# The last seam of a fused two-block kernel: the operand of up3 made from the output and a premultiplied residual, its pieces four tiles wide, up3 over six PSUM banks

## The chip, the cores and the metric

The kernel runs on one core of a Trainium2 chip. The metric is the device time of one launch in microseconds (us), lower is better. The engines are called by their short names: PE is TensorE, DVE is VectorE, ACT is ScalarE, POOL is GpSimd, SP is the engine that issues most transfers.

## What is computed

Two transformer-like blocks, one after the other, on 256 tokens of width 1024, all in float32. The change touches the place between the token mixer of the second block and its last feed-forward half:

```python
xs = xs + mod_x[5] * rmsnorm_2(y, g[3])          # y is the product with w_o ("o2")
xs = ffn_half(xs, mod_x[6], mod_x[7], mod_x[8], g[4], g[5], w_ff_in[l, 1], w_ff_out[l, 1])

def ffn_half(s, shift, scale, gate, g_pre, g_post, w_in, w_out):
    h = swiglu(modulate(rmsnorm_2(s, g_pre), shift, scale), w_in, w_out)
    return s + 0.5 * gate * rmsnorm_2(h, g_post)
```

So the output y of o2 is normalised and scaled by a gain row (g0 below), the residual is added, and the new residual is normalised, scaled by a second gain row (g1), turned to channels-major and multiplied with `w_ff_in` ("up3", 44 slabs of 128 columns: gate and up alternate) and then with `w_ff_out` ("down3").

## The kernel before

Every weight matrix comes as slabs of 128x1024 float32. For slab s, ACT rounds the raw slab into `hi` (the helper `split` on ACT) and DVE writes the remainder into `lo` (the helper `split` on DVE). Activations are held as `nh` and `nl` in the same way, and PE makes each product from three matmuls: nh*hi, nh*lo, nl*hi. There are HL = 3 slots of hi and lo, so slab s+3 can be split once slab s is used, and five slots of raw slabs, which SP fills in ring order. Nothing is scheduled automatically: each engine runs its instructions in the order in which the code issues them, and semaphores hold it where it has to wait. PE waits for `lo_done` before each slab (`begin`).

In the stage o2, the output has tokens on the partitions: PSUM banks 0 and 1 hold the two halves of token tile 0, banks 2 and 3 those of tile 1. The last two slabs of o2 are run bank by bank (`row_tail`), so that bank 0 is done first. For each bank, ACT squares it (`output_square`, a sum over the row comes with it); for each token tile ACT takes a root and DVE the inverse.

Before the change, DVE then multiplies each bank with g0 (`gained`), adds it with the inverse to the residual `xr` (`added_row`), and the new residual is multiplied with g1 into `xgr`: tile 0 by POOL, tile 1 by DVE (`next_gain`). PE transposes `xgr` in six pieces (`turned_rows`), ACT rounds each piece into `nh` (`pieces_rounded`) and DVE takes the remainder into `nl` (`piece_remainders`). The inverse norm of the new residual is not in that operand. It is applied to up3's results: ACT squares the new residual (`residual_square`), DVE makes a diagonal matrix of the inverse (`diagonal`), and PE multiplies it with ones (`inverse_rows`), which leaves the inverse in PSUM, along the columns (semaphore `stat`). DVE copies that to `rinv` and can only then take up3's first results. That is in `up` on DVE, and `up` on ACT holds the matching steps. Which slab these issue a split for, and where, matters here. In both kernels the split of slab 4 of up3 is issued in `up` of slab 1: on DVE behind all that takes in slabs 0 and 1, on ACT behind Silu of slab 0; and that Silu waits until DVE has multiplied slab 0 with `rinv`.

A second place is named below. Towards the end of the woven stage (positions p = 34 to 39 of its slabs), DVE scales the attention output `otok` (its line 2076, 128x2048), PE transposes pieces of it (`turn_out`, line 2789), and DVE takes the remainders of these pieces (line 2040, semaphore `o_lo`, on which the turns from the fourth on wait). POOL starts the transfer that broadcasts the gain rows g0, g1, g2 into `gain_rows` (line 686), which waits for the attention's last product.

Of the kernel before, what the change touches and what calls it, by code (L numbers as in the profile page):

```python
# [13 lines left out]
P = 128  # L14
D = 1024
# [6 lines left out]
BANKS = 4  # L22
# [31 lines left out]
def constants():  # L54
# [69 lines left out]
    "xg": dict(ffn1=2, pre2c=8, pre2x=6, mod2x=8, mod2c=8, rows2=2),  # L124
    "nh": dict(mix1=8, ffn1=6, pre2c=8, pre2x=8, mod2x=4, mod2c=4, pre3=7),
    "nl": dict(mix1=8, ffn1=6, pre2c=8, pre2x=8, mod2x=4, mod2c=4, pre3=7),
    "piece_made": dict(ffn1=6, pre2x=4, mod2x=4, mod2c=4, pre3=6),
# [30 lines left out]
PIECES_OF_PAIR = (2, 3, 5, 6)  # L158
# [58 lines left out]
def plan():  # L217
# [21 lines left out]
    st["up3"] = stage_slabs("up3", 2 * KH, cols=T + 2)  # L239
# [19 lines left out]
    for s, x in enumerate(work):  # L259
# [5 lines left out]
        if x.name == "v2" or x.name in ROWS:  # L265
            x.uses = list(uses)
            if x.j % 4 == 3 if x.name == "v2" else x.last:
                uses = [n + 1 for n in uses]
        else:
            x.use = uses[x.bank]  # L270
            uses[x.bank] += x.last and x.name != "in1"
# [7 lines left out]
def build(nc, d, out):  # L279
    st, work, ring = plan()  # L280
    with ExitStack() as ctx:
# [131 lines left out]
        squares = place(100 * KB, "squares", [P, 2, 512])  # L413
        diag = place(105 * KB, "diag", [P, 2, P])
# [41 lines left out]
        bank_free = [sem(f"bank_free{b}") for b in range(BANKS)]  # L456
# [54 lines left out]
        def _(pool):  # L511
# [178 lines left out]
            for b in range(2):  # L690
                w = slice(b * 512, b * 512 + 512)
                pool.wait_ge(sem("x"), since("x", "rows2") + b + 1)
                pool.tensor_tensor(xgr[:, 0, w], xr[:, 0, w], gain_rows[:, 1, w], ALU.mult)\
                    .then_inc(sem("xg_pool"), 1)


        @block.scalar
        def _(act):
# [14 lines left out]
            def prime(n, func):  # L713
                act.activation(idle[:, n:n + 1], cc("one"), func).then_inc(sem("primed"), 1)
# [62 lines left out]
            def pieces_rounded(m, between):  # L777


                if m == "pre3":  # L780

                    act.wait_ge(slab_used, st["o2"][-1].s + 1)
                    act.activation(nh[:, :, T:T + 2], mod[:, 6 * KD:7 * KD, 0:1].broadcast_to([P, KD, 2]), ACT.Copy)\
                       .then_inc(sem("nh"), 1)
                for n, (bank, k0, kn, tt) in enumerate(PIECES):
                    act.wait_ge(sem("piece_made"), since("piece_made", m) + n + 1)
# [3 lines left out]
                    if between and n == 1:  # L790
                        between()
# [18 lines left out]
            act.activation(idle[:, 6:7], small[:, 0:1], ACT.Copy).then_inc(sem("primed"), 1)  # L810
# [44 lines left out]
            for x in st["in1"]:  # L855
# [38 lines left out]
                if p == 10:  # L894
                    act.wait_ge(sem("c_landed"), 16)
                    act.activation(cvec[:, :, :], cvec[:, :, :], ACT.Silu).then_inc(sem("c_ready"), 1)
                    act.wait_ge(sem("u1_done"), Z1 + 3)
                    act.activation(u1[:, Z1:Z1 + 3, :], u1[:, Z1:Z1 + 3, :], ACT.Silu)\
                       .then_inc(sem("z_ready"), 1)
# [22 lines left out]
                if p == 17:  # L922
                    act.wait_ge(sem("ystat_ready"), 1)
                    act.activation(yroot[:, :, :], streams(ps[:, 5, :]), ACT.Sqrt, scale=1.0 / 192,
                                   bias=cc("eps")).then_inc(sem("yroot_ready"), 1)
# [41 lines left out]
            pieces_rounded("ffn1", None)  # L967
# [247 lines left out]
            for name in WOVEN:  # L1215
                for x in st[name]:
# [36 lines left out]
                    if p == 34:  # L1253
                        act.wait_ge(sem("oss_ready"), 2 * HEADS2)
                        act.activation(small[:, 208:224], small[:, 192:208], ACT.Sqrt, scale=1.0 / P,
                                       bias=cc("eps")).then_inc(sem("oroot_ready"), 1)
# [23 lines left out]
            for tt in range(2):  # L1280
                output_square(tt, 0)
                output_square(tt, 1)
                row_root("rows2", tt, tt + 1, 2 * tt + 2, SUM + 2 * tt + 1, PART + tt, ROOT + tt)
            residual_square(0, 0)
            split(st["o2"][-2].s + HL)
            pieces_rounded("pre3", None)
            split(st["o2"][-1].s + HL)
            residual_square(0, 1)
            row_root("rows2", 2, 3, 6, SUM + 5, PART + 2, ROOT + 2)
            residual_square(1, 0)  # L1290
# [18 lines left out]
        def _(dve):  # L1309
# [138 lines left out]
            def piece_remainders(m):  # L1448
# [1480 lines left out]
```

## Time and profile before

| | |
|---|---|
| median of 3 runs | 1268.71 us (1268.59 to 1270.02) |
| span of the profiled execution, from the first to the last instruction | 1265.3 us |
| median less that span | 3.4 us |
| PE busy, share of the span | 98% |
| DVE, ACT, POOL busy | 70%, 46%, 8% |
| mean granted clock of PE, share of full speed | 0.997 |

The profiled execution has no time of its own beside its span; the 3.4 us between the span and the median are what lies around the instructions. An engine's line in a timeline gives start, duration, engine, source line and operation, the tile written and those read, and in brackets how long the engine was idle before it and which instruction ended that. Durations of neighbouring instructions overlap a little, since each engine is pipelined.

### The profile page before, as it was taken

To read this page: it belongs to the slowest core of one execution; us is meant where nothing else is said; L and a number is where in the kernel's file an instruction comes from. 1 tells how busy PE (TensorE), PEld (TensorE's weight loads), DVE (VectorE), ACT (ScalarE), POOL (GpSimd) and SP (SyncE) were. 2 spreads that over 40 slices of the span, in tenths; PEclk is the share of its full clock that TensorE was granted. 3 is DMA by queue.
4 is the path that set the end of the run, shared out by engine and by line. 5 is a ranking of instruction groups with operands and counts; after the bars stand their busy time and mean duration, and the time that the engine had idled before them with its cause. 6 is when DMAs were issued, how large, how long until landed. Compare 5 with 4: busy or idle time off the path is not lost.

```text
span 1265.3 us, 19254 instructions
## 1 busy us (share of the span) xinstructions
PE 1235.7 (98%) x7645; PEld 1089.6 (86%) x7645; DVE 882.9 (70%) x1439; ACT 585.8 (46%) x927; POOL 100.6 (8%) x103
## 2 busy tenths in 40 slices
PE   6999999999999999999999999999999998999997
PEld 6987999978888888887787998888789997999986
DVE  5986889797787777753425776367886676777744
ACT  7656545545622222322325752246355645544533
POOL 2130001000000000001100022011420000000000
PEclk9999999999999999999999999999999999999999
DMA  7644777777366678853332543333233554655562
GB/s 288 209 139 150 233 235 242 234 242 238 112 217 200 199 251 282 293 189 107 110 133 75 167 150 100 100 117 116 86 101 100 200 167 139 193 180 181 179 195 84
DMA packets 59753, 219.28 MB, mean 173 GB/s; under 512 B 6844, under 2 KB 7136, under 8 KB 58896
## 3 DMA queue, kind: packets, MB, share of 16 engines
q1 hardware_dynamic: 56736, 205.42, 50.0%
q0 software_dynamic: 2352, 11.76, 2.7%
q8 instruction: 61, 1.00, 0.3%
q10 hardware_dynamic: 576, 0.88, 0.2%
q14 instruction: 28, 0.23, 0.1%
HBM read 216.95 MB, written 1.07 MB: 172 GB/s over the span
## 4 chain that ended last, share of the span: by engine, by line
PE 85%; DVE 6%; ACT 5%; issue 2%; DMA 1%; POOL 0%; DVEq 0%; ACTq 0%
PE ps L2182 19%; PE ps L2184 18%; PE ps L2183 18%; PE ps L2230 4%; PE ps L2232 4%; PE ps L2231 4%; PE ps L2241 3%; PE ps L2243 3%; PE ps L2242 3%; ACT hi L711 2%; PE ps L2220 1%; PE ps L2218 1%; PE ps L2219 1%; PE ps L2766 1%; DVE lo L1347 1%
## 5 line engine op out<-in xcount | busy, mean ns | idle before, releaser
L1347 DVE TENSOR_TENSOR lo<-raw,hi 128x1024 fp32r<-128x1024 f32 x315 | 388.5, 1234 | 247.5 <-ACT hi L711 244.4
L2182 PE MATMUL ps<-nh,hi 128*128 128x256 f32 (+2 forms) x1776 | 552.0, 311 | 4.5 <-DMA con<-in_consts 1.7
L711 ACT ACTIVATE hi<-raw 128x1024 fp32r<-128x1024 f32 x315 | 333.1, 1058 | 474.0 <-PE ps L2184 277.0
L2183 PE MATMUL ps<-nh,lo 128*128 128x256 f32 (+2 forms) x1776 | 544.2, 306 | 0.0
L2184 PE MATMUL ps<-nl,hi 128*128 128x256 f32 (+2 forms) x1776 | 544.1, 306 | 0.0
L2182 PEld LDWEIGHTS ps<-nh,hi 128*128 128x128 f32 x1776 | 338.4, 191 | 35.2 <-issue 15.7
L2183 PEld LDWEIGHTS ps<-nh,lo 128*128 128x128 f32 x1776 | 338.5, 191 | 16.5 <-issue 1.2
L2184 PEld LDWEIGHTS ps<-nl,hi 128*128 128x128 f32 x1776 | 338.3, 190 | 15.1
L1334 DVE SCALAR_TENSOR_TENSOR raw<-raw,cvec 128x1024 f32<-128x1024 f32 x72 | 86.8, 1222 | 1.4
L2230 PE MATMUL ps<-hi,H 128*128 128x512 f32 x176 | 69.1, 392 | 1.1 <-DVE lo L1347 1.1
L2241 PE MATMUL ps<-hi,H 128*128 128x512 f32 x176 | 69.4, 394 | 0.2 <-DVE ygx L1826 0.2
L2243 PE MATMUL ps<-hi,H 128*128 128x512 f32 x176 | 68.6, 390 | 0.0
L2231 PE MATMUL ps<-lo,H 128*128 128x512 f32 x176 | 68.5, 389 | 0.0
L2232 PE MATMUL ps<-hi,H 128*128 128x512 f32 x176 | 68.5, 389 | 0.0
L2242 PE MATMUL ps<-lo,H 128*128 128x512 f32 x176 | 68.5, 389 | 0.0
L1383 DVE TENSOR_TENSOR sg<-sg,ps 128x256 f32<-128x256 f32 (+1 forms) x44 | 24.3, 553 | 50.8 <-PE ps L2184 50.3
L1329 DVE SCALAR_TENSOR_TENSOR ps<-raw,cvec 128x1024 f32<-128x1024 f32 x40 | 49.0, 1226 | 0.0
L733 ACT ACTIVATE sg<-ps 128x512 f32<-128x512 f32 x22 | 13.1, 597 | 72.3 <-PE ps L2184 72.3
L2241 PEld LDWEIGHTS ps<-hi,H 128*128 128x128 f32 x176 | 33.0, 188 | 9.7 <-issue 2.9
L2230 PEld LDWEIGHTS ps<-hi,H 128*128 128x128 f32 x176 | 33.0, 188 | 9.5 <-DVE lo L1347 1.9
L1194 ACT ACTIVATE p<-ps,small 128x512 f32<-128x512 f32 x32 | 21.7, 684 | 41.3 <-DVE small L1994 41.3
L2243 PEld LDWEIGHTS ps<-hi,H 128*128 128x128 f32 x176 | 33.0, 188 | 7.0
(384 smaller groups left out, 1381.8 us busy)
## 6 DMA issues: line engine op xcount, KB each, us to landing
raw<-in_up SPq DMA_DIRECT2D x132, 512.0 KB, 3.7
raw<-in_in SPq DMA_DIRECT2D x86, 512.0 KB, 3.6
raw<-in_w_ada SPq DMA_DIRECT2D x72, 512.0 KB, 4.5
raw<-in_down SPq DMA_DIRECT2D x66, 512.0 KB, 3.7
raw<-in_out SPq DMA_DIRECT2D x8, 512.0 KB, 3.6
raw<-in_hy_out SPq DMA_DIRECT2D x8, 512.0 KB, 3.6
raw<-in_da_out SPq DMA_DIRECT2D x8, 512.0 KB, 4.0
raw<-in_o SPq DMA_DIRECT2D x8, 512.0 KB, 3.5
```

What stands on the lines that cost most here:

```text
L711: act.activation(hi[:, h, 0:n], raw[:, r, 0:n], ACT.Copy).then_inc(hi_done, 1)
L1334: dve.scalar_tensor_tensor(w, w, 1.0, cx, ALU.mult, ALU.mult, accum_out=mod[:, m:m + 1, s])\
L1347: dve.tensor_tensor(lo[:, h, 0:w], raw[:, r, 0:w], hi[:, h, 0:w].bitcast(F32), ALU.subtract).then_inc(lo_done, 1)
L2182: mm(o, hi[:, h, wk], x_hi, start=first, stop=False)
L2183: mm(o, lo[:, h, wk], x_hi, start=False, stop=False)
L2184: return mm(o, hi[:, h, wk], x_lo, start=False, stop=last)
L2230: mm(ps[:, b, :], x_hi, hi[:, h, w], start=x.first, stop=False)
L2231: mm(ps[:, b, :], x_hi, lo[:, h, w], start=False, stop=False)
L2232: return mm(ps[:, b, :], x_lo, hi[:, h, w], start=False, stop=x.last)
L2241: mm(ps[:, tt, :], x_hi, hi[:, h, w], start=x.first and j == 0, stop=False)
L2242: mm(ps[:, tt, :], x_hi, lo[:, h, w], start=False, stop=False)
L2243: o = mm(ps[:, tt, :], x_lo, hi[:, h, w], start=False, stop=x.last and j == 1)
```

## The change

1. POOL, once the gain rows have landed, multiplies g0 by g1 (`both_rows`, 128x1024) and the old residual by g1 into `xgr` (two instructions of 128x1024).
2. At the end of o2 DVE multiplies each bank with g0*g1 (`both_gained`, into `ygg`) and makes up3's operand as ygg * inverse + xgr (`next_operand`). The residual itself (`gained`, `added_row`) is made later, between the splits of up3's slabs. One of the four g0 products is done otherwise: ACT copies bank 1 to `yg` and POOL multiplies it.
3. PE transposes four pieces of four tiles each, in banks 4 to 7 (`turned_tiles`); ACT rounds them (`tile_rounded`), DVE takes the remainders in the order 0, 2, 1, 3 (`tile_remainders`).
4. up3 uses six banks (0, 1, 2, 3, 5, 6) and PE makes the inverse rows after four slabs of up3 (`x.j == 3`), not after two (`x.j == 1`).
5. The split of slab 3 of up3 is issued before `up`, in the seam; the split of slab 4 stays where it was, in `up` of slab 1.
6. Some semaphores are merged or dropped (`silu_done`, `root_ready`, `primed`).

```diff
-BANKS = 4
+BANKS = (0, 1, 2, 3, 5, 6)
...
+PIECES3 = ((4, 0, 0), (5, 4, 0), (6, 0, 1), (7, 4, 1))
+LOWS3 = (0, 2, 1, 3)
...
             pool.wait_ge(sem("gain_rows_landed"), 112)
-            for b in range(2):
-                w = slice(b * 512, b * 512 + 512)
-                pool.wait_ge(sem("x"), since("x", "rows2") + b + 1)
-                pool.tensor_tensor(xgr[:, 0, w], xr[:, 0, w], gain_rows[:, 1, w], ALU.mult)\
+            pool.tensor_tensor(both_rows[:, :], gain_rows[:, 0, :], gain_rows[:, 1, :], ALU.mult)\
+                .then_inc(sem("xg_pool"), 1)
+            pool.wait_ge(sem("yhy_ready"), KD)
+            for tt in range(2):
+                pool.tensor_tensor(xgr[:, tt, :], xr[:, tt, :], gain_rows[:, 1, :], ALU.mult)\
                     .then_inc(sem("xg_pool"), 1)
+            pool.wait_ge(bank_free[1], st["o2"][-1].uses[1] + 1)
+            pool.wait_ge(sem("xg"), since("xg", "rows2") + 4)
+            pool.tensor_tensor(yg[:, 0, 512:D], yg[:, 0, 512:D], gain_rows[:, 0, 512:D], ALU.mult)\
+                .then_inc(sem("xg_pool"), 1)
...
@@ ACT, up
-                    split(x.s + HL)
+                    if x.name == "up1" or x.j:
+                        split(x.s + HL)
...
@@ ACT, the seam
+            output_square(0, 0)
+            output_square(0, 1)
+            output_root(0)
+            output_square(1, 0)
+            act.wait_ge(sem("both_gained"), 2)
+            act.activation(yg[:, 0, 512:D], ps[:, 1, :], ACT.Copy).then_inc(bank_free[1], 1)
+            output_square(1, 1)
+            output_root(1)
+            shift_rounded()
+            tile_rounded(0)
+            split(st["o2"][-2].s + HL)
+            tile_rounded(1)
+            split(st["o2"][-1].s + HL)
             residual_square(0, 0)
...
+            split(st["up3"][0].s + HL)
+            residual_square(1, 0)
...
@@ DVE, up
-                    split(x.s + HL)
+                    if x.name == "up1":
+                        split(x.s + HL)
...
+            def both_gained(b):
+
+
+                dve.wait_ge(sem("sq"), since("sq", "rows2") + b + 1)
+                dve.tensor_tensor(piece(ygg, b), ps[:, b, :], both_rows[:, b % 2 * 512:b % 2 * 512 + 512],
+                                  ALU.mult).then_inc(sem("both_gained"), 1)
...
@@ PE
             for x in fed(st["up3"], "pre3"):
-                if x.j == 1:
+                if x.j == 3:
                     inverse_rows(2)
```

The change moves instructions on DVE, ACT, PE and POOL. First POOL, at the end of its program: the rows of the kernel before (names as in the code; `waits` lists the semaphores).

```order
L683 TENSOR_TENSOR proj<-proj 128x2x256 [waits folded]
L681 TENSOR_TENSOR ut<-spec_im 128x512
L683 TENSOR_TENSOR spec_im<-spec_im 128x2x256 [waits folded]
L686 DMA gain_rows<-gain_mem 128x3072 [waits o2_ready]
L693 TENSOR_TENSOR xgr<-xr,gain_rows 128x512 [waits x,gain_rows_landed]
L693 TENSOR_TENSOR xgr<-xr,gain_rows 128x512 [waits x]
L281 UNCONDITIONAL_BRANCH
```

And of the changed kernel, from the same transfer on:

```order
L691 DMA gain_rows<-gain_mem 128x3072 [waits o2_ready]
L695 TENSOR_TENSOR both_rows<-gain_rows 128x1024 [waits gain_rows_landed]
L699 TENSOR_TENSOR xgr<-xr,gain_rows 128x1024 [waits yhy_ready]
L699 TENSOR_TENSOR xgr<-xr,gain_rows 128x1024
L703 TENSOR_TENSOR yg<-yg,gain_rows 128x512 [waits xg,bank_free1]
L284 UNCONDITIONAL_BRANCH
```

Three instructions of 128x1024 now run as soon as the gain rows land, where before POOL was idle until the residual of the seam was there.

Next DVE in the seam, from the last split of o2 to the transposed pieces, in the kernel before:

```order
L1347 TENSOR_TENSOR lo<-raw,hi 128x1024 [waits hi_done] x5
L1405 TENSOR_SCALAR small<-small 128x1 [waits sq]
L2107 TENSOR_TENSOR yg<-ps,gain_rows 128x512 [waits sq] x2
L1410 RECIPROCAL small<-small 128x1 [waits root]
L2115 SCALAR_TENSOR_TENSOR xr<-yg,small,xr 128x512 [waits bank_free0,rinv]
L2115 SCALAR_TENSOR_TENSOR xr<-yg,small,xr 128x512 [waits bank_free1,rinv]
...
L2120 TENSOR_TENSOR xgr<-xr,gain_rows 128x512 [waits x] x2
L1453 TENSOR_TENSOR nl<-mod,nh 128x8x2 [waits nh]
L1458 TENSOR_TENSOR nl<-ps,nh 128x4x128 [waits nh]
```

In the changed kernel:

```order
L1378 TENSOR_TENSOR lo<-raw,hi 128x1024 [waits hi_done] x5
L1437 TENSOR_SCALAR small<-small 128x1 [waits sq,xg_pool]
L2164 TENSOR_TENSOR ygg<-ps,both_rows 128x512 [waits sq]
L2149 TENSOR_TENSOR yg<-ps,gain_rows 128x512 [waits sq]
L2164 TENSOR_TENSOR ygg<-ps,both_rows 128x512 [waits sq]
L1442 RECIPROCAL small<-small 128x1 [waits root]
L2172 SCALAR_TENSOR_TENSOR xgr<-ygg,small,xgr 128x512 [waits both_gained,rinv] x2
...
L2164 TENSOR_TENSOR ygg<-ps,both_rows 128x512 [waits sq] x2
L1442 RECIPROCAL small<-small 128x1 [waits root]
L2172 SCALAR_TENSOR_TENSOR xgr<-ygg,small,xgr 128x512 [waits both_gained,rinv] x2
L1491 TENSOR_TENSOR nl<-mod,nh 128x8x2 [waits nh]
L1501 TENSOR_TENSOR nl<-ps,nh 128x4x128 [waits nh] x4
```

The row L2120 between the new residual and the transposes is gone, and so is POOL's work there.

Last DVE between the second diagonal and the first splits of up3. Before (`diag` is the diagonal, `sg` the gate, COPY rinv is the first to wait for `stat`):

```order
L1445 TENSOR_SCALAR diag<-con,small 128x128 [waits rinv]
L1347 TENSOR_TENSOR lo<-raw,hi 128x1024 [waits hi_done]
L1358 COPY rinv<-ps 128x256 [waits stat]
L1363 COPY small<-ps 128x1 [waits slab_used,dve_step]
L1364 TENSOR_TENSOR sg<-ps,rinv 128x256
L1370 COPY small<-ps 128x1 [waits slab_used]
L1371 TENSOR_TENSOR sg<-ps,rinv 128x256
L1374 SCALAR_TENSOR_TENSOR sg<-sg,small 128x256 [waits gate_open,dve_step]
L1347 TENSOR_TENSOR lo<-raw,hi 128x1024 [waits hi_done]
```

In the changed kernel:

```order
L1477 TENSOR_SCALAR diag<-con,small 128x128 [waits rinv]
L1390 COPY rinv<-ps 128x256 [waits stat]
L1395 COPY small<-ps 128x1 [waits slab_used,dve_step]
L1396 TENSOR_TENSOR sg<-ps,rinv 128x256
L1402 COPY small<-ps 128x1 [waits slab_used]
L1403 TENSOR_TENSOR sg<-ps,rinv 128x256
L1406 SCALAR_TENSOR_TENSOR sg<-sg,small 128x256 [waits gate_open,dve_step]
L1378 TENSOR_TENSOR lo<-raw,hi 128x1024 [waits hi_done]
```

The first `lo` of the rows before is the split of slab 3 of up3 and has moved up into the seam; the second is that of slab 4, and it still stands behind the row that waits for `stat`.

## Rows read from the trace of the kernel before

**Rows 1.** The page: busy us, share of the span, instructions.

```profile
PE 1235.7 (98%) x7645; PEld 1089.6 (86%) x7645; DVE 882.9 (70%) x1439; ACT 585.8 (46%) x927; POOL 100.6 (8%) x103
```

**Rows 2.** Timeline of PE in the seam, from the last matmul of o2.

```profile
1061.86 0.39 PE L2232 MATMUL ps<-hi,nl 128*128 128x512 f32 x1
1063.77 0.63 PE L2307 MATMUL ps<-con,xgr 128*128 128x128 f32 x4 [1.52 <-POOL xgr L693]
1066.73 2.82 PE L2307 MATMUL ps<-con,xgr 128*128 128x128 f32 x12 [2.33 <-DVE xgr L2120]
1069.20 0.56 PE L2182 MATMUL ps<-nh,hi 128*128 128x258 f32 x1
...
1069.99 0.32 PE L2182 MATMUL ps<-nh,hi 128*128 128x258 f32 x1
```

**Rows 3.** Timeline of ACT in the seam.

```profile
1060.92 0.60 ACT L758 ACTIVATE squares<-ps 128x512 f32<-128x512 f32 x1 [0.28 <-PE ps L2232]
...
1063.06 0.29 ACT L766 ACTIVATE small<-small 128x1 f32<-128x1 f32 x1
...
1064.93 0.57 ACT L787 ACTIVATE nh<-ps 128x512 fp32r<-128x512 f32 x1
```

**Rows 4.** Timeline of DVE in the seam.

```profile
1059.14 0.15 DVE L1405 TENSOR_SCALAR small<-small 128x1 f32<-128x1 f32 x1
...
1061.08 1.41 DVE L2115 SCALAR_TENSOR_TENSOR xr<-yg,small,xr 128x512 f32<-128x512 f32 x2
...
1062.48 1.28 DVE L2107 TENSOR_TENSOR yg<-ps,gain_rows 128x512 f32<-128x512 f32 x2
```

**Rows 5.** Stretches of time: busy us by engine, then granted clock, DMA.

```profile
1062.30:1069.20 6.90, 3.10 (x16) 2.90 (x17) 6.39 (x13) 4.35 (x11) 2.56 (x2) 0.81 0.00 0
1066.60:1070.00 3.40, 3.27 (x16) 3.27 (x17) 2.76 (x8) 2.04 (x6) 0.00 (x0) 0.50 0.02 5
123.00:127.00 4.00, 2.88 (x21) 2.13 (x20) 3.97 (x8) 3.87 (x10) 0.57 (x1) 1.00 0.08 31
1261.00:1263.00 2.00, 0.00 (x0) 0.00 (x0) 1.24 (x3) 0.00 (x0) 0.00 (x0) 0.55 0.35 129
```

**Rows 6.** Timeline of PE around the inverse rows (L2315).

```profile
1075.42 0.61 PE L2315 MATMUL ps<-diag,con 128*128 128x128 f32 x4
1075.79 0.36 PE L2182 MATMUL ps<-nh,hi 128*128 128x258 f32 x1
```

**Rows 7.** Timeline of DVE and ACT, from the copy of rinv on.

```profile
1077.47 0.42 DVE L1358 COPY rinv<-ps 128x256 f32<-128x256 f32 x1
...
1078.87 1.04 ACT L711 ACTIVATE hi<-raw 128x1024 fp32r<-128x1024 f32 x1
1079.94 1.23 DVE L1347 TENSOR_TENSOR lo<-raw,hi 128x1024 fp32r<-128x1024 f32 x1 [0.39 <-ACT hi L711]
```

**Rows 8.** The gain rows' transfer (KB, us to landing), and who then works.

```profile
994.53 0.58 POOL L686 DMA_DIRECT2D gain_rows<-gain_mem  x1 [63.50 <-PE ps L2745]
gain_rows<-gain_mem POOLq DMA_DIRECT2D x1, 1536.0 KB, 8.6
1003.60 2.29 DVE L2076 TENSOR_TENSOR otok<-otok,small 128x2048 f32<-128x2048 f32 x1
1005.95 0.66 PE L2789 MATMUL ps<-con,otok 128*128 128x128 f32 x4 [0.21 <-DVE otok L2076]
...
1012.62 0.60 PE L2789 MATMUL ps<-con,otok 128*128 128x128 f32 x4
```

**Rows 9.** Timeline of POOL and DVE where both run at once.

```profile
757.62 1.29 POOL L658 TENSOR_TENSOR kre<-kre 128x512 f32<-128x512 f32 x1
758.30 1.68 DVE L1347 TENSOR_TENSOR lo<-raw,hi 128x1024 fp32r<-128x1024 f32 x1 [1.92 <-ACT hi L711]
...
900.95 2.22 POOL L681 TENSOR_TENSOR ut<-proj 128x512 f32<-128x512 f32 x1
901.94 1.39 DVE L1986 CUSTOM_DVE_ANT_0 rtmp<-otok 128x128 f32<-128x128 f32 x1
```

More of the change, by code:

```diff
@@ L238, in plan @@
     st["o2"] = row_slabs_of("o2", KD)
-    st["up3"] = stage_slabs("up3", 2 * KH, cols=T + 2)
+    st["up3"] = stage_slabs("up3", 2 * KH, cols=T + 2, banks=BANKS)
     st["down3"] = row_slabs_of("down3", KH)
@@ L413, in build @@
         squares = place(100 * KB, "squares", [P, 2, 512])
+        both_rows = place(82 * KB, "both_rows", [P, D])
+        ygg = place(34 * KB, "ygg", [P, 2, D])
         diag = place(105 * KB, "diag", [P, 2, P])
@@ L455, in build @@
         ada_used = sem("ada_used")
-        bank_free = [sem(f"bank_free{b}") for b in range(BANKS)]
+        bank_free = {b: sem(f"bank_free{b}") for b in BANKS}
         block = ctx.enter_context(nc.Block())
@@ L713, in prime @@
             def prime(n, func):
-                act.activation(idle[:, n:n + 1], cc("one"), func).then_inc(sem("primed"), 1)
+                act.activation(idle[:, n:n + 1], cc("one"), func)
             def got(x):
@@ L775, in bank_done, with pieces_rounded @@
                     act.wait_ge(slab_used, x.s + 1)
[L777 to L784, printed above, removed]
+            def pieces_rounded():
                 for n, (bank, k0, kn, tt) in enumerate(PIECES):
[L786 removed]
+                    act.wait_ge(sem("piece_made"), since("piece_made", "ffn1") + n + 1)
                     act.activation(nh[:, k0:k0 + kn, tt * P:tt * P + P],
@@ L789, in pieces_rounded, with shift_rounded, tile_rounded @@
                        .then_inc(sem("nh"), 1)
-                    if between and n == 1:
-                        between()
+            def shift_rounded():
+                act.wait_ge(slab_used, st["o2"][-1].s + 1)
+                act.activation(nh[:, :, T:T + 2], mod[:, 6 * KD:7 * KD, 0:1].broadcast_to([P, KD, 2]), ACT.Copy)\
+                   .then_inc(sem("nh"), 1)
+            def tile_rounded(tt):
+                for n in (2 * tt, 2 * tt + 1):
+                    bank, k0, _ = PIECES3[n]
+                    act.wait_ge(sem("piece_made"), since("piece_made", "pre3") + n + 1)
+                    act.activation(nh[:, k0:k0 + 4, tt * P:tt * P + P],
+                                   ps[:, bank, :].rearrange("p (k n) -> p k n", k=4), ACT.Copy)\
+                       .then_inc(sem("nh"), 1)
             def square(m, k, src, scale=1.0):
@@ L809, in _ @@
             act.wait_ge(sem("dve_step"), 1)
-            act.activation(idle[:, 6:7], small[:, 0:1], ACT.Copy).then_inc(sem("primed"), 1)
+            act.activation(idle[:, 6:7], small[:, 0:1], ACT.Copy)
             act.wait_ge(sem("par_landed"), 16)
@@ L2301, in turned_rows, with turned_tiles @@
                     if tt:
-                        pe.wait_ge(sem("xg"), gains + k0 // 4 + 1)
+                        pe.wait_ge(sem("xg"), since("xg", "ffn1") + k0 // 4 + 1)
                     else:
-                        pe.wait_ge(sem("xg_pool"), pooled + k0 // 4 + 1)
+                        pe.wait_ge(sem("xg_pool"), k0 // 4 + 1)
                     for j in range(kn):
+                        k = (k0 + j) * P
+                        o = pe.transpose(ps[:, bank, j * P:j * P + P], xgr[:, tt, k:k + P], ident)
+                    o.then_inc(sem("piece_made"), 1)
+            def turned_tiles():
+                for n, (bank, k0, tt) in enumerate(PIECES3):
+                    pe.wait_ge(sem("xg"), since("xg", "rows2") + n + 1)
+                    for j in range(4):
                         k = (k0 + j) * P
```

104 lines of the change are left out of this document (57 added, 47 removed).

## The prediction

> **What bounds the kernel now.** I read the page first: PE is busy 98% of the span [rows 1], so what counts is any stretch in which PE stands still or runs at the lower clock, and anything that adds such a stretch. In the timeline of PE at the seam [rows 2] the last matmul of o2 starts at 1061.86 and ends at 1062.25; the first of up3 starts at 1069.20. These 6.95 us hold 16 transposes and two waits, 1.52 us for POOL's and 2.33 us for DVE's product with g1. The stretch view [rows 5] adds the clock: from 1066.6 to 1070.0 it is granted at 0.50, that is 1.2 GHz, after 4.4 us in which PE did four transposes. Twelve transposes start 0.2 us apart there (2.82 us), four at the full clock 0.12 us apart (0.63 us), so they lose 12 x 0.085 = 1.0 us; up3's first three matmuls take 0.79 us in place of 0.36, 0.45 us lost. The seam at 123 to 127 us, of the same kind but with PE busy 2.88 of 4 us, kept the clock at 1.00 [rows 5].
>
> **Part 1, the new chain at the seam.** I lay the new order of DVE and ACT over the old times. DVE is free at 1059.14 [rows 4]. Each product from PSUM is followed after 0.60 us (two take 1.28 [rows 4]): ygg 0, yg 0, ygg 1 end at 1061.1. The inverse of tile 0 and two scalar_tensor_tensor of 0.70 each (1.41 for two [rows 4]) put the operand of tile 0 at 1061.9 and 1062.6, so PE transposes tile 0 straight after o2. For tile 1: two products to 1063.9, inverse, two operands done at 1064.7 and 1065.4. ACT's added copy of bank 1 (about 0.6) fits between its squares, one starting at 1060.92, and the last root still starts at 1063.06 [rows 3]. PE's third piece starts at 1064.75 and is done at 1065.4; ACT rounds it (0.57 [rows 3]) to 1066.0; DVE's remainder (0.7, priced as a product from PSUM) to 1066.75. up3 waits for tiles 0 and 2 only and starts at about **1066.85, 2.35 us sooner**. The fourth piece's remainder is done near 1068.0, and PE needs it 12 matmuls later, at 1068.3. POOL's last product (1.3 us from 1065.45) lies beside DVE's reads of PSUM.
>
> The residual work that is moved (four additions, two products, four squares) goes between splits. I followed it: the low parts of slabs 1, 2, 3 are ready at 1069.1, 1070.9, 1074.5, and PE wants them at 1069.75, 1072.65, 1075.55; the second diagonal is ready at 1077.85, PE wants it at 1078.45. It costs nothing while PE covers it, with 0.6 us to spare at the tightest places.
>
> **Part 2, the inverse after four slabs.** This is the edit that the profile speaks against. From the fourth matmul of up3 (1069.99 [rows 2]) to the inverse rows (1075.42 [rows 6]) 45 matmuls pass in 5.43 us, 0.121 each: a slab of 24 is 2.9 us. The inverse rows take 0.61 until their end, 0.37 until PE goes on [rows 6]. Before, two slabs follow (5.8 us), and under them DVE copies rinv, takes slabs 0 and 1 in, ACT runs Silu and rounds slab 4, DVE makes its low part: from 1077.47 to 1079.94 + 1.23 = 1081.17, **3.70 us** [rows 7]. PE begins slab 4 at 1075.79 + 5.8 = 1081.6, so the chain was hidden. In the changed order the same rows stand behind the same wait for `stat`, but the slab that PE wants next is slab 4 itself. Six banks let PE write slab 4; its weights are not there. With up3 started at 1066.85: four slabs to 1078.45, inverse done 1079.05, chain to 1082.75, slab 4 begins at 1082.8. That is **1.2 us later than before**, with PE idle 3.75 us. The gain of the seam (2.35, and 0.45 of slow matmuls that this sum leaves out) is spent here with 4.0 us against it. Later slabs keep up: two splits of 1.23 and the short instructions of a pair take DVE some 4 us, and PE 5.8. The six banks themselves save nothing: PE is not seen to wait for a bank in up3.
>
> **Part 3, POOL's three wide products.** They run once the gain rows land: 994.53 + 8.6 = 1003.13 [rows 8]. DVE starts its 2.29 us product on otok at 1003.60, and PE waits for exactly that at 1005.95 [rows 8], so every delay of it goes to the end. Does POOL delay DVE? The row at 758.30 says yes: `lo`, usually 1.23, took 1.68 when it began 0.68 us after a POOL product of 1.29 [rows 9]; and at 900.95 a POOL product waited for DVE's, then the DVE instruction behind it, of only 128x128, took 1.39. Both have all inputs in SBUF; the products from PSUM beside POOL were not lengthened [rows 4]. POOL has 512 columns in these rows. At 1024 I take twice the 1.29 row less one overhead, 2.4 us (bounds: nothing, if POOL comes too late, and 2.6). Then POOL holds 1003.2 to 1005.5, otok runs to 1007.8, PE is **1.9 us** late. POOL's second product takes the next turn, then DVE's low part of slab 38, then POOL's third, then slab 39. The first remainders of otok's pieces stand behind slab 39 on DVE and are done at 1015.2 and 1015.6 (three POOL turns and two splits after otok, then a product and two remainders of 0.4). PE wants the first at 1012.62 + 1.9 = 1014.5 [rows 8], so another **1.0 us**. Sum +2.9. If the transfer lands after 1003.6, DVE goes first, otok is on time, and only the remainders are late: +1.4 by the same walk.
>
> The Trainium skill, page "SBUF — State Buffer", section "Who interferes with whom", says that a DVE instruction with two SBUF inputs and a POOL instruction that reads SBUF exclude each other, and the one that comes second waits until the first is finished. By that rule the wide product would cost otok its whole length, +2.9 in the sum; if the 1024-wide product cost only what the 512-wide ones show (0.45 to 1.1), the sum would be +0.5 to +1.5.
>
> **Part 4, the clock.** In the changed seam PE is busy about 2.4 us of the 4.6 before up3, between the two seams of [rows 5]: it may keep the full clock. The idle 3.75 us before slab 4 has no matmul at all, and at the kernel's end, with PE idle, the grant is 0.55 between 1261 and 1263 [rows 5]. A fall costs what the rows show: 3.4 us at half rate are at most 1.7 us of work, less what of it falls into idle time. I take one fall, **1.3 us**; bounds 0 and 3.4 (both places, whole).
>
> **The sum**, against the profiled execution: 1265.3 + 1.2 + 2.9 + 1.3 = 1270.7, and with the 3.4 us that lie between this span and the median, 1274.1. Merged semaphores cost nothing: each waits for what its engine had done long before.
>
> **Rivals.**
> (a) Only the stall, POOL hidden: for it, PE is some slabs behind DVE's splits, so most of what POOL delays has slack; against it, otok has none [rows 8]. 1268.7 + 1.2 + 1.3 = 1271.2 (1269.9 to 1273.3).
> (b) The other side: slab 4's split is not late, since ACT and DVE get through the copy, Silu and rounding earlier than I read. Then only the seam counts: 2.35 + 0.45 saved: 1268.7 - 2.8 = 1265.9 without POOL's cost, 1268.8 with it. It decides if the 3.70 us chain fell under 1 us, for which no row speaks, since the wait for `stat` stands ahead of it.
> (c) More of everything: the clock falls twice, or POOL gets two turns ahead of otok (DVE's reciprocal ahead of it blocked): 1274.1 + 2.1 = 1276.2 or more.
> (d) No change that shows: gain and stall cancel, POOL costs 1 us or less, clock kept: about 1269.5.
>
> **How the numbers follow.** The forecast 0.50 with its own range 1272.3 to 1276 (POOL +1.4 and a cheap fall, to both falls); (a) 0.22; (c) 0.10; (d) 0.10; (b) 0.08. The range 1269.8 to 1276.3 leaves out (b), part of (c) and the lower edge of (d), some 0.2. A measurement of this kernel tells 0.2%, 2.5 us, from no change. Slower by more: the forecast, (c) and half of (a) and a bit, 0.72; within: the rest of (a), (d), half of (b), 0.21; faster 0.07.
>
> **What the changed profile would show.** Right: no wait of PE for POOL or DVE `xr` at the seam and up3 starting about 4.6 us after o2's last matmul; a PE wait of 3.5 to 4 us for DVE's `lo` ahead of slab 4; otok ending more than 1.5 us after its start plus 2.29, with POOL's row before it, and a PE wait for it of about 2 us, then one for `nl` of about 1 us. Wrong: slab 4's low part ahead of the copy of rinv in time; POOL's products after otok; or a clock that stays at 1.00 throughout. The sum is most at risk in the moment at which the gain rows land, 0.5 us ahead of otok.

## The result, and the profile after

| | kernel before | changed kernel |
|---|---|---|
| median, same chip | 1269.05 us (1268.06 to 1270.20, 6 runs) | 1275.44 us (1272.85 to 1279.45, 6 runs) |
| ratio, 95% interval | | 1.0059, 1.0049 to 1.0068 |
| span of the profiled execution | 1265.3 us | 1276.0 us |

The change makes the kernel slower: by 0.59%, 7.5 us, by the ratio of the runs, and by 6.4 us by the two medians. The forecast was 1274.1, 5.4 us slower, with a range to 1276.3; the ratio times the 1268.7 of before gives 1276.2, and times the 1269.05 of this comparison 1276.5. The direction and the places were right, the size came out at the upper edge or just over it.

The page and, of the waits of PE, the rows that are new, larger, or in the place of an old one (engine, tile, line <- what it waited for: us in total, times, longest):

```profile
PE 1241.4 (97%) x7645; PEld 1093.9 (86%) x7645; DVE 890.9 (70%) x1442; ACT 586.8 (46%) x926; POOL 109.6 (9%) x105
...
PE ps L2243 <- DVE lo L1378: 4.7, 4, 3.8
PE ps L2860 <- DVE otok L2118: 1.7, 1, 1.7
PE ps L2378 <- DVE xgr L2172: 1.5, 1, 1.5
PE ps L2243 <- DVE nl L1501: 0.8, 1, 0.8
PE ps L2860 <- DVE nl L2082: 0.7, 1, 0.7
```

The number of PE's instructions is that of [rows 1], but they are busy for 5.7 us more: the same matmuls ran longer. That is the mark of a lower clock. The largest wait is that for `lo`, then that for `otok`; the 1.52 and 2.33 us of the old seam [rows 2] have become one of 1.5 and one of 0.8.

The timeline of PE at the places of the sum:

```profile
1009.59 0.66 PE L2860 MATMUL ps<-con,otok 128*128 128x128 f32 x4 [1.67 <-DVE otok L2118]
...
1066.55 0.39 PE L2293 MATMUL ps<-hi,nl 128*128 128x512 f32 x1
1066.78 1.22 PE L2378 MATMUL ps<-con,xgr 128*128 128x128 f32 x8
1069.47 1.32 PE L2378 MATMUL ps<-con,xgr 128*128 128x128 f32 x8 [1.46 <-DVE xgr L2172]
1071.63 0.55 PE L2243 MATMUL ps<-nh,hi 128*128 128x258 f32 x1 [0.85 <-DVE nl L1501]
...
1084.56 0.61 PE L2386 MATMUL ps<-diag,con 128*128 128x128 f32 x4
1088.95 0.58 PE L2243 MATMUL ps<-nh,hi 128*128 128x258 f32 x1 [3.79 <-DVE lo L1378]
...
1208.16 0.40 PE L2293 MATMUL ps<-hi,H 128*128 128x512 f32 x1
1208.95 0.51 PE L2291 MATMUL ps<-hi,H 128*128 128x512 f32 x1 [0.40 <-DVE sg L1406]
```

The last two lie at the start of down3. The same two of the kernel before:

```profile
1198.14 0.39 PE L2232 MATMUL ps<-hi,H 128*128 128x512 f32 x1
1198.37 0.39 PE L2230 MATMUL ps<-hi,H 128*128 128x512 f32 x1
```

Set against [rows 2, 6, 8] these give an account of the 10.7 us by which this execution's span is longer:

| from, to | how much later | worked out |
|---|---|---|
| start to 125 us | +2.13 | the start, in this execution (below) |
| to the last matmul of o2 | +2.56 | 1066.55 - 1061.86 - 2.13: POOL |
| to the first matmul of up3 | -2.26 | 1071.63 - 1066.55 = 5.08, before 7.34: the seam |
| to the inverse rows | +0.91 | 12.93 in place of 6.22 + 5.8: the clock after the seam |
| to slab 4 | +4.02 | 4.39 in place of 0.37: the stall of 3.79, and 0.2 of restart |
| to 1100 us | +2.65 | PE's matmuls of that time are 10.01 later in all: the clock after the stall |
| to the end | +0.69 | 10.7 - 10.01: the start of down3 |

The last row is no cost of the clock. The four PSUM banks that down3 writes are 0 to 3. With four banks the last of up3's 44 slabs lies in bank 3, which down3 wants fourth; with six it lies in bank 1, which down3 wants second, and PE waits until DVE has taken the slab out (its row `sg`, line 1406). The first matmul of the second bank starts 0.79 us after the one ahead of it in place of 0.23, and the next loses 0.1 more. The trace of every kernel with six banks has this loss, e6's among them, and e5's, with four banks, has none. No run has the six banks alone, so the cause is read from the code and the wait, not shown by an experiment.

The stretch view shows the two falls of the clock in up3 (columns as in [rows 5]), then the rest at the full clock:

```profile
1071.00:1074.20 3.20, 2.57 (x12) 2.60 (x13) 3.20 (x5) 1.36 (x2) 0.49 (x1) 0.51 0.02 5
1084.00:1095.00 11.00, 7.21 (x38) 7.02 (x38) 7.73 (x18) 5.01 (x8) 0.00 (x0) 0.69 0.40 126
1088.95:1095.00 6.05, 6.05 (x28) 6.05 (x29) 4.66 (x11) 2.30 (x4) 0.00 (x0) 0.50 0.72 230
1095.00:1250.00 155.00, 154.60 (x1118) 147.08 (x1118) 101.77 (x173) 73.72 (x97) 0.00 (x0) 1.00 0.55 182
```

A grant of 0.69 over 11 us is 11 x 0.31 / 0.5 = 6.8 us at 1.2 GHz, twice the 3.4 us of the one fall before the change [rows 5]. By the third row 6.0 us of it lie on slabs 4 and 5, and so 0.8 us in the stall. The first row holds 12 matmuls in 2.57 us, 0.215 each, where 0.121 is the pace at 2.4 GHz; 28 matmuls at the slower pace behind the stall are 2.6 us lost, which is the 2.65 of the account.

The 2.13 us at the start have nothing to do with the change. Between 12 and 20 us this execution had the clock at 0.79, and so had the profiled executions of six of the twelve runs below; there PE's matmuls at 125 us are 1.2 to 2.1 us later than in the profile before, in the other six 0.0 to 0.8. Kernels with the change are in both groups. That is one source of the spread of about 3 us between runs of one kernel.

```profile
12.00:20.00 8.00, 6.24 (x36) 6.03 (x35) 3.38 (x5) 5.77 (x13) 4.80 (x6) 0.79 0.75 298
```

Now POOL and DVE, the timelines around `otok`:

```profile
1004.44 2.95 POOL L695 TENSOR_TENSOR both_rows<-gain_rows 128x1024 f32<-128x1024 f32 x1 [7.14 <-DMA gain_rows<-gain_mem]
1007.37 7.77 POOL L699 TENSOR_TENSOR xgr<-xr,gain_rows 128x1024 f32<-128x1024 f32 x2
...
1003.89 1.23 DVE L1378 TENSOR_TENSOR lo<-raw,hi 128x1024 fp32r<-128x1024 f32 x1 [0.99 <-ACT hi L721]
1005.04 0.42 DVE L2077 TENSOR_TENSOR tT<-gT,ps 128x256 f32<-128x256 f32 x1
...
1005.80 3.74 DVE L2118 TENSOR_TENSOR otok<-otok,small 128x2048 f32<-128x2048 f32 x1
1009.46 3.41 DVE L1378 TENSOR_TENSOR lo<-raw,hi 128x1024 fp32r<-128x1024 f32 x1
1012.80 0.41 DVE L2077 TENSOR_TENSOR tT<-gT,ps 128x256 f32<-128x256 f32 x1
1013.13 3.09 DVE L1378 TENSOR_TENSOR lo<-raw,hi 128x1024 fp32r<-128x1024 f32 x1
```

The two engines take turns. POOL's first product is issued at 1004.44, inside DVE's split of 1003.89, and is stretched to 2.95 us; it ends at 1007.39. DVE's `otok` is issued at 1005.80 and ends at 1009.54, which is 1007.39 + 2.15, or its usual length [rows 8] within 0.14 us. The next two splits take 3.41 and 3.09 in place of 1.23: each waits for a product of POOL. The two short rows `tT` have one input in PSUM and keep their 0.42 us with POOL running. The Trainium skill, page "SBUF — State Buffer", section "Who interferes with whom", says that an instruction of DVE with two SBUF inputs and one of POOL that reads SBUF exclude each other for the whole instruction, and that one of DVE with at most one SBUF input does not contend (two-port modes of DVE left aside); these rows agree with both halves.

Last the chain behind the inverse, DVE and ACT:

```profile
1085.20 0.42 DVE L1390 COPY rinv<-ps 128x256 f32<-128x256 f32 x1 [2.73 <-PE ps L2386]
...
1086.19 0.51 ACT L735 ACTIVATE sg<-sg,small 128x256 f32<-128x256 f32 x1 [2.71 <-DVE sg L1396]
1086.60 1.04 ACT L721 ACTIVATE hi<-raw 128x1024 fp32r<-128x1024 f32 x1
...
1087.67 1.23 DVE L1378 TENSOR_TENSOR lo<-raw,hi 128x1024 fp32r<-128x1024 f32 x1 [0.39 <-ACT hi L721]
```

From the copy to the end of slab 4's low part it is 3.70 us, exactly as before [rows 7]. DVE stood idle for 2.73 us ahead of the copy and ACT for 2.71 us ahead of Silu: they had time for slab 4's split, but it stood behind the wait.

How long the clock stays low is not the same in every execution of this kernel. The mean granted clock was recorded for all six: the fastest, 1272.85 us, had 0.998, the others 0.996, 0.996, 0.995, 0.993 (the profiled one) and 0.994 at 1273.94, 1275.06, 1275.83, 1277.78 and 1279.45 us. Over the span, 0.998 is 3.8 to 6.4 us at 1.2 GHz. The last stretch of the kernel takes 0.9 to 4.1 of these in the profiled executions, so the fastest had no 6.8 us behind its stall.

### The profile page after: what moved, and what is told of

The parts are those of the page before. It is cut to its first block, busy times and chain, and to the rows that moved or that the text cites. A ratio compares the mean times of both kernels' runs of the same rounds, so it can differ in the third digit from the quotient of the medians.

```text
span 1276.0 us, 19259 instructions
## 1 busy us (share of the span) xinstructions
PE 1241.4 (97%) x7645; PEld 1093.9 (86%) x7645; DVE 890.9 (70%) x1442; ACT 586.8 (46%) x926; POOL 109.6 (9%) x105
## 4 chain that ended last, share of the span: by engine, by line
PE 84%; DVE 7%; ACT 5%; issue 3%; DMA 1%; POOL 0%; DVEq 0%; ACTq 0%
PE ps L2243 19%; PE ps L2244 18%; PE ps L2245 18%; PE ps L2291 4%; PE ps L2292 4%; PE ps L2293 4%; PE ps L2302 3%; PE ps L2304 3%; PE ps L2303 3%; ACT hi L721 2%; DVE lo L1378 1%; PE ps L2281 1%; PE ps L2280 1%; PE ps L2279 1%; PE ps L2837 1%
## 5 line engine op out<-in xcount | busy, mean ns | idle before, releaser
L1378 DVE TENSOR_TENSOR lo<-raw,hi 128x1024 fp32r<-128x1024 f32 x315 | 392.7, 1247 | 245.7 <-ACT hi L721 242.5
```

The costliest lines, as they stand in the source:

```text
L1378: dve.tensor_tensor(lo[:, h, 0:w], raw[:, r, 0:w], hi[:, h, 0:w].bitcast(F32), ALU.subtract).then_inc(lo_done, 1)
```

## The experiments

Twelve runs were made, of ten different kernels, in four batches; each ratio is against the kernel before on the same chip (medians 1268.39, 1268.50, 1267.34 and 1267.93 us). Where two experiments are compared across batches, their ratios are. All carry the whole computation; some add work whose result nobody reads. The cuts are shortened. E numbers are in the order of running.

### 1. The stall alone: e6 and e1

Is the inverse after four slabs dear by itself? e6 is the kernel before with only edit 4, six banks and the inverse after four slabs (and the merged semaphores):

```diff
-BANKS = 4
+BANKS = (0, 1, 2, 3, 5, 6)
...
             for x in fed(st["up3"], "pre3"):
-                if x.j == 1:
+                if x.j == 3:
                     inverse_rows(2)
```

> The kernel before, with up3 over six banks and the inverse rows after four slabs; the seam as it was. Theory: the 3.7 us chain from stat to slab 4's low part is uncovered, PE idle 3.8 us there, and the clock falls after it at a cost of 1.5 to 3 us: 5 to 7 us slower than the kernel before. Rival (six banks give back what the stall takes): 3 us slower or less.

Measured: 1275.52 us (5 runs), ratio 1.0059 (1.0046 to 1.0072). Its timeline of PE and the stretch after:

```profile
1087.58 0.58 PE L2182 MATMUL ps<-nh,hi 128*128 128x258 f32 x1 [3.79 <-DVE lo L1347]
...
1084.00:1095.00 11.00, 7.42 (x40) 7.42 (x41) 8.26 (x19) 6.05 (x9) 0.00 (x0) 0.69 0.46 144
```

The stall is the same to the hundredth, 3.79 us, and so is the 0.69: 6.8 us at 1.2 GHz, 5.75 of them behind the stall. Edit 4 alone costs 7.5 us, as much as the whole change, and more than the 5 to 7 expected: the clock, and the 0.7 us at the start of down3, which no expectation had. The seam's gain of 2.3 and POOL's cost of 2.6 nearly cancel beside it.

e1 is the changed kernel with the splits of slabs 4 and 5 ahead of the wait for `stat`, so that the stall has no cause (the conditions that take these splits out of the other places of `up` are left out of the cut):

```diff
@@ ACT, up
-                    if x.name == "up1" or x.j:
+                    if x.name == "up1" or x.j > 2:
                         split(x.s + HL)
@@ ACT, the seam, behind the squares
+            for x in st["up3"][1:3]:
+                split(x.s + HL)
@@ DVE, the seam, behind the diagonals
+            for x in st["up3"][1:3]:
+                split(x.s + HL)
```

> The changed kernel with the splits of slabs 4 and 5 of up3 issued ahead of the wait for stat. Theory (stall plus clock): PE no longer waits 3.8 us before slab 4, and the clock no longer falls there, so the time drops by 3.8 us plus 1.7 to 3.4 us, to about 1 us over the kernel before (1269.5 to 1271). Rival (the stall has another cause, say the copy of rinv or the banks): a PE wait of 2 us or more stays before slab 4, 5 or 6 and the drop is under 2 us.

Measured: 1270.23 us (11 runs), ratio 1.0016 (1.0008 to 1.0025). The waits for `lo` in up3 shrink, the clock stays at 1.00 from the seam to PE's last matmul, and POOL's cost is untouched:

```profile
PE ps L2248 <- DVE lo L1381: 2.4, 5, 1.2
PE ps L2865 <- DVE otok L2121: 2.1, 1, 2.1
```

0.39 us is left ahead of slab 4 and 1.17 ahead of slab 6. The ratio falls by 0.0043, 5.5 us (3.0 to 7.6 by the two intervals), where the waits fall by no more than 3.79 - 1.56 = 2.2. So the stall brought a cost beside its length.

### 2. The clock behind the stall: e4 and e10

Here PE does more work, not less: 28 transposes of the unit matrix into a bank that nobody reads, in the stall. Nothing else starts sooner.

```diff
                 if x.j == 3:
                     inverse_rows(2)
+                    for _ in range(28):
+                        pe.transpose(ps[:, 4, 0:P], ident, ident)
```

e4 puts them into the changed kernel.

> The changed kernel with 28 transposes of a constant into an unused bank between the inverse rows and slab 4, 3.4 us of PE work inside the 3.8 us stall, and nothing else. Theory (the clock falls because PE stands still, and that costs 1.7 to 3.4 us on top of the stall): no fall of the clock after slab 4 begins, 2 to 3 us less than the changed kernel although PE does more. Rival (the clock falls for other reasons, or the loss after slab 4 is not the clock): the same time as the changed kernel, or more.

Measured: 1272.01 us (1270.95 to 1272.83, 5 runs), ratio 1.0030 (1.0018 to 1.0042), 3.7 us less than the changed kernel (0.9 to 6.3 by the two intervals). Timeline and stretch:

```profile
1082.90 3.22 PE L2903 MATMUL ps<-con 128*128 128x128 f32 x28
1086.86 0.39 PE L2243 MATMUL ps<-nh,hi 128*128 128x258 f32 x1 [0.73 <-DVE lo L1378]
...
1084.00:1095.00 11.00, 10.27 (x88) 10.03 (x87) 9.82 (x21) 7.56 (x11) 0.00 (x0) 1.00 0.54 168
```

The stall is as long as it was (3.2 us filled, 0.7 waited), but the clock stays at 1.00 and slab 4's first matmul takes 0.39 in place of 0.58.

e10 does the same to e6, where neither seam nor POOL is changed.

> The kernel before with the inverse rows after four slabs over six banks (7.0 us slower than before when measured), and 28 transposes of a constant in the stall. It parts the 7.0 us into the stall and the clock: theory, 4.0 to 4.3 us slower than the kernel before, with no fall of the clock after slab 4 begins; the other 3 us were the clock. Rival (the clock's part is small, as the forecast's 1.3 us): 5.5 us slower or more.

Measured: 1272.55 us (5 runs), ratio 1.0038 (1.0026 to 1.0051), against 1.0059 without the transposes; again the clock is 1.00 behind the stall. So of the 7.5 us of edit 4, 0.0021, 2.7 us, are the clock, and 4.8 us are what does not hang on it: the stall with its restart, 4.0 us in e6's trace, and the 0.7 at the start of down3. The measured 4.8 us lie between the 4.0 to 4.3 expected and the rival's 5.5. The two intervals overlap a little (1.0046 and 1.0051) and the runs were on different chips, so the times alone do not prove the difference. The clocks do not rest on that: the traces have 0.69 against 1.00 over the same 11 us, and of the five executions of each kernel none of e6 has a mean granted clock above 0.994 and none of e10 one below 0.996. The 2.6 us lost by 28 matmuls in the account above are of the same size as the 2.7.

### 3. POOL: e5, e2, e3, e7

e5 is the kernel before with the three products of POOL added, where the change has them. Their results go to places that nobody reads, and the output is made as before.

```diff
             pool.wait_ge(sem("gain_rows_landed"), 112)
+            pool.tensor_tensor(both_rows[:, :], gain_rows[:, 0, :], gain_rows[:, 1, :], ALU.mult)\
+                .then_inc(sem("early"), 1)
+            pool.wait_ge(sem("yhy_ready"), KD)
+            for tt in range(2):
+                pool.tensor_tensor(xgr[:, tt, :], xr[:, tt, :], gain_rows[:, 1, :], ALU.mult)\
+                    .then_inc(sem("early"), 1)
```

> The kernel before, with POOL's three wide products added where the changed kernel has them (their results are not used) and the semaphores merged as there. Theory (POOL and DVE shut each other out around otok, whatever the seam does): 2 to 3 us slower than the kernel before, a PE wait of about 1.7 us for otok and 0.7 us for the remainders, nothing at the seam. Rival (the cost only showed because of the run's other shifts): under 1 us slower.

Measured: 1270.32 us (11 runs), ratio 1.0016 (1.0008 to 1.0025), 2.0 us slower (1.0 to 3.2). Timeline, POOL and then DVE, and the stretch of PE behind the wait:

```profile
1004.01 2.40 POOL L691 TENSOR_TENSOR both_rows<-gain_rows 128x1024 f32<-128x1024 f32 x1 [8.42 <-DMA gain_rows<-gain_mem]
...
1004.09 4.46 DVE L2084 TENSOR_TENSOR otok<-otok,small 128x2048 f32<-128x2048 f32 x1
...
1009.91:1013.32 3.41, 3.41 (x18) 3.41 (x17) 3.41 (x3) 0.02 (x1) 3.41 (x2) 0.50 0.15 28
```

POOL is 0.08 us ahead, takes its 2.40 us alone, and `otok` is twice as long as in [rows 8]; PE waits 2.4 us for it. The phase of the two engines differs between executions, from 1.67 to 2.39 us of wait. Behind the longest of these waits the clock fell too, for 3.4 us, and PE does not wait for the remainders; this execution is 3.7 us late at the end of o2, more than the runs' 1.0 to 3.2.

e2 holds the products back in the changed kernel until the woven stage's last slab is used:

```diff
             pool.wait_ge(sem("gain_rows_landed"), 112)
+            pool.wait_ge(slab_used, st["da_out"][-1].s + 1)
```

> The changed kernel with POOL's three wide products held until the last slab of da_out is used. Theory (DVE and POOL shut each other out): otok takes 2.3 us again, PE's waits of 1.7 us for otok and 0.7 us for the remainders go, 2.5 us less than the changed kernel, the stall of 3.8 us stays. Rival (POOL costs little, the shift at otok comes from the start of the run): less than 1 us less.

Measured: 1275.02 us (6 runs), ratio 1.0059 (1.0046 to 1.0072), the same as the changed kernel. The 2.5 us less that were expected did not come. The wait for `otok` is gone, but the products now meet DVE at 1041.5 to 1049.8, where it prepares the first slabs of o2:

```profile
1041.80 2.35 DVE L2139 TENSOR_TENSOR tT<-tT,tda 128x256 f32<-128x256 f32 x1
1044.08 3.43 DVE L1379 TENSOR_TENSOR lo<-raw,hi 128x1024 fp32r<-128x1024 f32 x1
1047.43 2.95 DVE L2128 TENSOR_TENSOR nl<-tT,nh 128x256 fp32r<-128x256 f32 x2
...
PE ps L2292 <- DVE lo L1379: 2.9, 3, 1.1
```

This row `tT` has both inputs in SBUF, unlike the one above, and takes 2.35 us in place of 0.42. PE loses 2.4 us here where the changed kernel lost 2.56 at `otok`: the cost was moved, not removed. The same trace has the bare stall, and a fall of the clock half as long as in the changed kernel:

```profile
1086.22 0.58 PE L2244 MATMUL ps<-nh,hi 128*128 128x258 f32 x1 [3.79 <-DVE lo L1379]
...
1084.00:1095.00 11.00, 8.78 (x61) 8.79 (x62) 8.77 (x18) 6.73 (x10) 0.00 (x0) 0.84 0.53 159
```

A grant of 0.84 over 11 us is 3.5 us at 1.2 GHz, nearly all of it behind the stall, and PE loses 1.5 us by it, not 2.65. The six executions of e2 have mean clocks from 0.998 to 0.993, as those of the changed kernel.

e3 has the edits of e1 and of e2. The two savings were expected to add.

```diff
+            pool.wait_ge(slab_used, st["da_out"][-1].s + 1)
...
+            for x in st["up3"][1:3]:
+                split(x.s + HL)
```

> Both edits of the two runs before. Theory: the savings add, since they lie at two places of PE's line: only the seam's gain of about 2.3 us is left, and what the clock adds or gives; 1266 to 1268, faster than the kernel before by 1 to 3 us. Rival (the seam itself gains nothing that PE can use): same as the kernel before within 1 us.

Measured: 1270.13 us (11 runs), ratio 1.0014 (1.0006 to 1.0023), not told apart from e1, and slower than the 1266 to 1268 expected: e2's edit saves nothing here either.

e7 holds the products back a little longer, to a stretch in which DVE has only the splits of o2:

```diff
+            pool.wait_ge(slab_used, st["o2"][0].s + 1)
```

> The changed kernel with POOL's three wide products held until the first slab of o2 is used, where DVE has only splits that are three slabs ahead of PE; the run that held them until da_out had ended lost as much at the start of o2 as it won at otok. Theory: no PE wait for otok beyond 0.2, none new in o2, 2.5 us less than the changed kernel. Rival (the cost moves with the products wherever they go): as the changed kernel, within 1 us.

Measured: 1271.70 us (7 runs), ratio 1.0029 (1.0017 to 1.0040), 3.8 us less than the changed kernel by the ratios, more than the 2.56 us that its rows had given (the intervals allow 1.2 to 6.4). POOL works, and PE waits for nothing new:

```profile
1044.07 2.43 POOL L696 TENSOR_TENSOR both_rows<-gain_rows 128x1024 f32<-128x1024 f32 x1 [48.27 <-PE ps L2294]
1046.47 6.71 POOL L700 TENSOR_TENSOR xgr<-xr,gain_rows 128x1024 f32<-128x1024 f32 x2
...
PE ps L2244 <- DVE lo L1379: 4.7, 4, 3.8
PE ps L2292 <- DVE lo L1379: 1.1, 1, 1.1
```

DVE's splits are blocked here as well (three of them take 7.58 us together), but PE does not need them yet. The stall of 3.8 us is still there, and with it 6.8 us at the half clock, 5.3 of them behind the stall.

### 4. Both costs out: e8, e9, e11, e12

e8 is the changed kernel with POOL as in e7, and the splits of slabs 4, 5 and 6 ahead of the wait for `stat`; ACT rounds slab 4 right behind slab 3, so that DVE finds it ready.

```diff
+            pool.wait_ge(slab_used, st["o2"][0].s + 1)
@@ ACT, the seam
             split(st["up3"][0].s + HL)
+            split(st["up3"][1].s + HL)
             residual_square(1, 0)
...
+            for x in st["up3"][2:4]:
+                split(x.s + HL)
@@ DVE, the seam, behind the diagonals
+            for x in st["up3"][1:4]:
+                split(x.s + HL)
```

> The changed kernel with POOL's products in o2 and the splits of slabs 4, 5 and 6 of up3 ahead of the wait for stat, ACT's of slab 4 sooner still. Theory (the seam's gain of 2.3 us is real and only hidden): PE waits in up3 under 0.4 us in sum, 2 to 3 us faster than the kernel before. Rival (something else of the change costs): no faster than the kernel before.

Measured: 1266.30 us (11 runs), ratio 0.9984 (0.9975 to 0.9992). The longest wait for `lo` in up3 is 0.5 us, and the clock holds from the seam to PE's last matmul:

```profile
1062.00:1071.00 9.00, 6.70 (x49) 5.58 (x48) 8.94 (x16) 6.36 (x14) 1.27 (x1) 1.00 0.13 35
1071.00:1095.00 24.00, 23.53 (x196) 23.33 (x195) 20.88 (x47) 15.71 (x27) 0.00 (x0) 1.00 0.56 184
...
PE ps L2250 <- DVE lo L1383: 1.4, 4, 0.5
```

Of the four waits three, 0.9 us, are in the kernel before as well, outside up3. The loss at the start of down3 is still there.

e9 adds ten transposes in the seam's wait of 1.46 us, as a cover against a fall there (the changed kernel's execution had one, e8's none):

```diff
+                    if n == 1:
+                        for _ in range(10):
+                            pe.transpose(ps[:, 7, 0:P], ident, ident)
```

> The run before (splits early, POOL in o2) with ten transposes of a constant into bank 7 between the second and third piece of the seam, 1.2 us of PE work inside a 1.5 us wait. If the clock still falls at the new seam in a good share of executions, this is 0.3 to 1 us faster and its times spread less; if the seam mostly keeps the clock by itself, it is the same within 0.3 us.

Measured: 1267.13 us (11 runs), ratio 0.9996 (0.9987 to 1.0005). No gain; but it was on another chip than e8. So both ran once more side by side, e11 as e8 and e12 as e9.

> The same kernel as the one with POOL's three products in o2 and the splits of slabs 4, 5 and 6 ahead of the copy of rinv (0.9984 of before on another chip), now on one chip with the next kernel. If its gain was real: ratio 0.998 to 0.999 again (1.3 to 2.5 us faster than before). Rival, that the gain was the chip's spread of runs: 0.9995 to 1.001.

> The same kernel as the one that has ten filling transposes in the seam as well (0.9996 before, on another chip), beside the kernel without them on one chip. If the fill does nothing but take PE's idle time: the ratio of the kernel without it, within 0.0007. Rival, that the fill costs PE about 1.2 us or keeps it from starting in time: 0.001 above that kernel's ratio.

Measured: e11 1266.91 us, ratio 0.9989 (0.9980 to 0.9998); e12 1265.52 us, ratio 0.9982 (0.9974 to 0.9991), 11 runs each. The order of the two turned round (e12's ratio is below e11's by 0.0007, e9's had been above e8's by 0.0012), so the transposes in the seam make no difference that these runs can tell. Of four ratios three lie wholly under 1, their mean is 0.9988: the repaired change, with the filling transposes or without, is about 1.5 us faster than the kernel before. That is less than the 0.2% that a single comparison tells from no change, but seen in three of four.

## Why the prediction was right, and where it was not

**Part 1, the seam.** Right. up3 was to start 4.6 us after the end of o2's last matmul and did so after 1071.63 - 1066.94 = 4.69; the gain was 2.26 for 2.35. What covers the moved residual work held too: no wait for slabs 1 to 3. Where the new seam keeps the clock, up3 gains the slow matmuls besides, which the sum left out: in e8's trace 0.4 us.

**Part 2, the stall.** Right to a few hundredths: 3.79 us idle for 3.75, the chain 3.70 for 3.70. e6 shows it without anything else of the change, and e1 that it goes when the split stands ahead of the wait. Rival (b) is out.

**Part 3, POOL.** Right in mechanism, 2.56 us for 2.9. PE was 1.5 us late at `otok` for 1.9, since POOL's first product ended about 0.3 us sooner against DVE than the walk had it. The remainders of the pieces added 1.05 for 1.0. The value taken for 1024 columns, 2.4 us, is what e5 and e7 show (2.40 and 2.43). e5 and e7 bear out that this costs time and can be avoided; rival (a), POOL hidden, is out.

**Part 4, the clock.** This step failed, by its size: "I take one fall, **1.3 us**; bounds 0 and 3.4 (both places, whole)". The two places were the right ones, and in the profiled execution the clock fell at both. The seam's fall makes four slabs take 12.93 us where the prediction's walk has 11.6, 1.3 us; the one at the stall cost 2.65; together 4.0, above the bound. What failed is the length that it gave to a fall: 3.4 us, as in [rows 5], and less what of it lies in idle time. At the bare stall it was 6.8 us in the changed kernel, e6 and e7, of which only 0.8, 1.1 and 1.5 us lay in the idle time. In e2, with the same stall, it was 3.4, at a cost of 1.5 us; there 1.3 would have been near. e4 and e10 show the part behind the stall as a cost of its own: 3.7 and 2.7 us less, with a stall of the same length and more work for PE. What decides between the short fall and the long one is not shown.

The seam's fall was in the changed kernel's profile, but not in those of e1, e2, e3, e4, e7, e8 and e11, which have the same seam; the old seam has one in all four profiles that contain it (the kernel before, e5, e6, e10). That both falls differ between executions would explain why the ratio says 7.5 us and this execution, without its start, 8.6. The single profiles do not prove that share.

**The six banks.** "The six banks themselves save nothing" is right for up3, but their cost was put at nothing without a look at down3. It is 0.7 us, by the two pairs of rows at 1208 and 1198 us.

With 2.65 in place of 1.3 for the clock, one fall, and 0.7 for down3, the forecast's own sum would have been 1265.3 + 1.2 + 2.9 + 2.65 + 0.7 + 3.4 = 1276.2, the lower of the two measured values. That it meets it to the tenth is luck, since the falls vary. Rival (c), in which the clock falls twice and the time is 1276.2 or more, had a chance of 0.10 and is nearest to what the profiled execution shows.

One term of the base was misread, at no cost to the sum. The 3.4 us between the span and the median were taken as time around the instructions. Every run for which both are listed, of this kernel and of the others, has about 1.8 us between its time and its span. If that held in the profiled execution of the kernel before, it took about 1267.1 us, and the other 1.6 us are that it was a fast one.

The Trainium skill, page "TensorE: Matmul & The Clock Gate", section "HAM oscillation — how this bites in real kernels", tells of waits that are long enough for the array to cool, so that the work behind them starts at the half rate. The stretches agree: 3.79 us idle, then 1.2 GHz; the same 3.9 us with transposes in them, then 2.4 GHz. In e5 a wait of 2.39 us was followed by 1.2 GHz as well. The prediction counted the fall, but took its length from one that followed a seam in which PE had been partly busy.

## What to carry to other kernels

When a wait is moved, look at what is queued behind it on its engine, and put what doesn't need it ahead: here a weight split behind a copy cost 4 us, with the engine idle before it. When a ring of banks or buffers is made longer, look at where the last user leaves it: the next stage may want that very one first. A stall of the matrix engine has two prices, its length and the clock behind it; the second was 1.5 to 2.7 us behind a stall of 3.8, and differs between executions, so one profile does not give it. A test with idle transposes in the stall measures it apart. "Idle" POOL time is no free room when DVE works on two SBUF inputs: put such products where DVE has slack over the whole of their length, not merely elsewhere.

## What the runs showed of the hardware that was not expected

- At the bare stall of 3.79 us the clock fell in four traces of four. It was low for 6.8 us in three of them, although PE was busy for the last 6.0, 5.75 and 5.3 us of it, and for 3.4 us in the fourth (e2).
- It fell for 3.4 us behind a wait of 2.39 us (e5) and in the old seam (four traces of four), and in one of the eight traces that have the new seam without transposes in it.
- Twenty-eight transposes that do nothing, 3.22 us, ahead of a last wait of 0.7 us kept it at 1.00, in two traces of two; no execution of these two kernels has a mean clock below 0.996, where the changed kernel and e6 go down to 0.993 and 0.992.
- Two inputs in SBUF or one decides for short DVE instructions too: `tT` of 128x256 takes 0.42 us beside POOL with one input in PSUM, and 2.35 us with both in SBUF.
- POOL is blocked as well: the two wide products after the first take 7.77 us together in the changed kernel and 6.71 us in e7, where one alone takes 2.4.
